# Moving the head norm's squared root to two idle buffers, and the last third of the rotation table into the value stage

## The chip, the core and the metric

The kernel runs on one core of one Trainium2 chip. The metric is the time of one execution on the device in microseconds (us); several runs are made and their median is given. Lower is better.

## What is computed

Four transformer layers in a row on 256 latent tokens and 256 context tokens of width 1024, all in 32-bit floats. The first layer, where most of the change acts, is cut here to what matters:

```python
def rms_norm(x, g):
    y = x * rsqrt(mean(x * x, axis=-1) + 1e-6)
    return y * g

# layer 0: neighbourhood attention; w = na_wqkv, 16 heads of 64
ql, kl, vl = split((u_lat @ w).reshape(B, L, 3, H, dh))
qc, kc, vc = split((u_ctx @ w).reshape(B, C, 3, H, dh))
ql, qc, kl, kc = (rms_norm(t, gain) for t in (ql, qc, kl, kc))   # per head of 64
# layer 1: sliding window attention, q and k normed per head in the same way, then rotated
# layer 2: s5_mixer, a diagonal complex state space model:
a_bar = exp(lam * dt)          # its powers, chunk by chunk, are the "rotations" below
```

The modulation vectors of layers 0 and 1 come from `silu(c) @ ada_w[i] + ada_b[i]`, a matrix-vector product with 96 slabs of 128 outputs each.

## The kernel before

Everything is written for the raw engines: each engine runs one list of instructions in order and waits on semaphores. The work is cut into **stages** (`make_plan`), each a matrix product whose output comes in tiles of 128 features. `qk0` makes the 16 query and key tiles of layer 0 over 512 tokens, `v0` its values in 8 weight units, then comes the attention of layer 0 (`ATT0`). `q1` (8 tiles of 256 tokens), `k1` (2 tiles of 512) and `v1` are the same for layer 1. A 32-bit product is three matmuls: operand and weight are each split into a high and a low part (L699 to L701; L764 to L766 in a value stage).

**A weight unit** (128x1024) is loaded by SyncE into one of four `raw` slots (L546). ScalarE copies it to `w_hi` (L1127, `split_unit`), VectorE makes `w_lo` (L1554, `lower`), three units ahead of TensorE.

**A query or key tile** of the stages `qk0`, `q1` and `k1` takes this path (`b2` is the tile's parity, for two sets of buffers):

1. ScalarE squares the bank of products into `sq[b2]` (L1145, "the Square").
2. TensorE sums the squares per head with a matmul against a constant (`sum_tile`, L777).
3. ScalarE: `tmp` from the sums (L1259), logarithm (L1131), exponential (L1132), which is the root `y` in `rs[b2]`, and the root squared (L1261), written to the same `sq[b2]` as the squares of step 1.
4. VectorE copies the products out (L1596) and applies one Newton step and the gain (`qk_scale`, L1748 to L1750). L1748 reads the squared root. Its end is semaphore `d2`.

Since the squared root of tile j lies in `sq[b2]` until L1748 has read it, the Square of tile j+2 waits for `d2` of tile j. ScalarE's order is: `w_hi` copy, Square of tile j, then the root (step 3) of tile j-1. The root of tile j waits for `d2` of tile j-2 as well, because of `tmp` and `rs`. TensorE's order in `qk0` and `q1` goes by groups of four tiles. Within a group the sum of a tile follows the products of the next one; at the group's end the sums of its last two tiles stand one behind the other, so the first product of the next group stands behind the last Square of this one.

**VectorE's list** in `qk0` has per tile: `lower`, a product of one `ada` slab for every second tile (`ada_unit`, L1566 and L1567), the copy and the Newton step, and one step of `rotations(u)`, u being the tile: the table `rot0` of powers for layer 2, doubled step by step (`rot_double`, L1978 to L1984). In `v0` it has `lower` and one or two `ada` slabs per unit. The `ada` slabs come through two buffers, each loaded again (L541) when its product is done. TensorE waits before the attention for the last `ada` product of `v0`, which writes to a bank that the attention uses.

**GpSimd** (POOL) only issues transfers here, in order: `pw` and `bbar` to DRAM, constants, `rot0` to DRAM (L2241, 1.5 MB), then 16 bias tiles for the attention (L2252): the first four when `qk0` is done, the others as the attention frees them. `rot0` lies where the attention puts its probabilities, so ScalarE waits for `pre_saved` (all three tables stored) before `v0`.

`rsn` and `ssum` are the buffers of the whole-row norm, which is not running while `qk0`, `q1` and `k1` do.

Of the kernel before, what the change touches and what calls it, by code (L numbers as in the profile page):

```python
# [154 lines left out]
def program(nc, weights, ada_w, ada_b, x_t, vecs, cons, bias_na, ssm_in, ssm_bc, scratch, out):  # L155
# [5 lines left out]
    with ctx:  # L161
# [39 lines left out]
        ssum = place("ssum", [P, TOK])  # L201
        tmp = place("tmp", [P, 2, TOK])
        half_eps = place("half_eps", [P, 1])
        whole_eps = place("whole_eps", [P, 1])
# [136 lines left out]
        ss0, x_in, pre_cout, pre_zero = sem("ss0"), sem("x_in"), sem("pre_ca_out"), sem("pre_zero")  # L341
        pre_saved, tab_loaded, bc_loaded, zero_set = sem("pre_saved"), sem("tab_loaded"), sem("bc_loaded"), sem("zero_set")
        gain_done = sem("gain_done")
# [767 lines left out]
        def _(act):  # L1111
# [4 lines left out]
            A = act.activation  # L1116
# [17 lines left out]
            def tile(s, i, jj, body, first=False):  # L1134
# [4 lines left out]
                if s.kind == "QK":  # L1139

                    act.wait_ge(S["unit"], n_done)
                    act.wait_ge(S["p2"], value("p2", s, j - 1))
                    if s.name not in LATE:
                        act.wait_ge(S["d2"], value("d2", s, j - 1))
                    A(sq[:, b2, 0:s.tok], bank[:, 0:s.tok], ACT.Square).then_inc(S["a1"], 1)  # L1145
# [106 lines left out]
            def qk_root(s, i, jj, body):  # L1252
                j = i * body + jj
                b2 = (s.tile0 + jj) % 2

                act.wait_ge(S["p2"], value("p2", s, j + 1))
                act.wait_ge(S["d2"], value("d2", s, j - 1))
                v, y = tmp[:, b2, 0:s.tok], rs[:, b2, 0:s.tok]
                chain.link(A(v, (SS, SS2)[b2][:, 0:s.tok], ACT.Identity, bias=half_eps[:, :], scale=-0.5 * INV_HD))  # L1259
                chain.link(root(y, v))  # L1260
                A(sq[:, b2, 0:s.tok], y, ACT.Square).then_inc(S["a2"], 1)  # L1261

# [184 lines left out]
            stage("qk0")  # L1447
            act.wait_ge(pre_saved, 48)
            stage("v0")
            attention(ATT0, 0)  # L1450
            stage("wo0"); norm(1, "mlp0")
# [88 lines left out]
        def _(dve):  # L1540
# [199 lines left out]
            def qk_scale(s, i, jj, body):  # L1740
# [5 lines left out]

                v, y, y2_ = tmp[:, b2, 0:s.tok], rs[:, b2, 0:s.tok], sq[:, b2, 0:s.tok]
                link(TT(v, v, y2_, ALU.mult))  # L1748
# [5 lines left out]
            def stage(name):  # L1754
# [10 lines left out]
                def one(i, first=False, last=False):  # L1765
                    for jj in range(body):
# [25 lines left out]
                        if s.name == "qk0":  # L1792
                            rotations(i * 4 + jj)
                    if s.kind == "QK" and s.name in LATE:
                        if i == 1:
                            late_mean(s, 7)
                            late_scale(s, 6)
                            late_scale(s, 7)
                    elif s.kind == "QK":
                        qk_scale(s, i, body - 1, body)  # L1800
# [185 lines left out]
            def rotations(u):  # L1986
# [13 lines left out]
                elif 4 <= u < 8:  # L2000
                    rot_double(2 ** (u - 4))
                elif u in (8, 9):
                    rot_double(16, re=(u == 8), im=(u == 9))
                elif u == 12:
                    link(dve.tensor_copy(rot0[:, 2, :, :], v(7).unsqueeze(2).to_broadcast([P, PAIRS, NCH])))
# [224 lines left out]
        def _(pool):  # L2230
# [8 lines left out]
            pool.dma_start(con[:, N_EARLY:], cons[:, N_EARLY:]).then_inc(late_in, 16)  # L2239
            pool.wait_ge(pre_v, 5)  # L2240
            pool.dma_start(rot_dram, rot0[:, :, :, :]).then_inc(pre_saved, 16)  # L2241
            chain = Chain(pool, pool_chain)
            link = chain.link

            for b in range(HEADS):
                if b == 0:

                    stage_end(pool, ST["qk0"], ("d2",))
                if b >= 4:
                    pool.wait_ge(att_m, 2 * (b - 4) + 2)  # L2250
# [8 lines left out]
            stage_end(pool, ST["up0b"], ("unit", "d1"))  # L2259
            pool.wait_ge(pre_saved, 48)  # L2260
            def table_inputs(H, js):
# [215 lines left out]
```

## Time and profile before

| | us |
|---|---|
| median of 3 runs | 1752.43 |
| lowest and highest run | 1748.91, 1753.97 |
| the profiled execution's own time | 1750.73 |
| its span (first to last instruction) | 1748.9 |
| mean granted TensorE clock, share of full speed | 0.968 |
| busy: TensorE matmul / VectorE / ScalarE | 1627.1 / 1312.5 / 870.6 |

The stages that the change touches lie in this stretch of the span: `qk0` from 44 to 162 us, `v0` from 162 to 208, the attention of layer 0 from 210; `q1` from 718 to 758, `k1` to 772, `v1` to 789, the attention of layer 1 from 792.

In the rows below PE is TensorE's matmul part, DVE is VectorE, ACT is ScalarE. A bracket at a row's end, `[1.99 <-DVE qk L1750]`, says how long the engine had been idle before the instruction and which instruction it had waited for. The idle time of an engine that nobody waits for costs nothing.

### The profile page before, as it was taken

Reading aid. Unit: us, or ns where it says so; the run is one execution under the profiler, and the core shown is the slowest. Engines: PE = TensorE matmul, PEld = TensorE weight load, DVE = VectorE, ACT = ScalarE, POOL = GpSimd, SP = SyncE. Lnnn points to the kernel's source line nnn. Section 1 sums busy time; section 2 is a strip of 40 time slices with the busy share of each in tenths; the row PEclk is TensorE's granted clock in tenths of the full one; section 3 lists DMA queues with packets and bytes.
Section 4 is the critical chain, followed back from the end, with each engine's and each line's share of the span. In section 5 each row is a group of like instructions: output and inputs, shape, how many; then the busy total and the mean of one; then the engine's idle time right before and its main releaser. Section 6 shows DMA issues by size and latency. Waiting matters only on the chain.

```text
span 1748.9 us, 32745 instructions
## 1 busy us (share of the span) xinstructions
PE 1627.1 (93%) x11892; PEld 1435.7 (82%) x11892; DVE 1312.5 (75%) x2239; ACT 870.6 (50%) x1497; POOL 96.5 (6%) x152
## 2 busy tenths in 40 slices
PE   5899999899999999698989999689999989799999
PEld 3677866688888888584789999689999988599999
DVE  4899797788767877678677786777887666468874
ACT  4555387343213433556555555155555576455552
POOL 0001030000000023100001212100000000000000
PEclk9899999999999999898999999799999999899999
DMA  9236651435657855320256768525555544045554
GB/s 359 87 108 228 217 140 43 145 119 187 200 192 239 264 177 167 106 94 13 66 183 203 220 200 304 234 97 174 186 180 192 183 143 145 1 156 180 182 192 142
DMA packets 79626, 290.74 MB, mean 166 GB/s; under 512 B 10000, under 2 KB 11792, under 8 KB 77600
## 3 DMA queue, kind: packets, MB, share of 16 engines
q1 hardware_dynamic: 69120, 249.03, 43.0%
q0 software_dynamic: 10400, 40.30, 7.0%
q8 instruction: 67, 1.10, 0.3%
q14 instruction: 39, 0.32, 0.1%
HBM read 270.61 MB, written 18.68 MB: 165 GB/s over the span
## 4 chain that ended last, share of the span: by engine, by line
PE 75%; DVE 14%; ACT 6%; issue 4%; DMA 2%; ACTq 0%; DVEq 0%; SPq 0%; POOLq 0%
PE bank L699 21%; PE bank L701 21%; PE bank L700 21%; DVE stat L2069 2%; PE bank L764 1%; PE bank L766 1%; PE bank L765 1%; ACT w_hi L1127 1%; DVE w_lo L1554 1%; DVE prob L2088 1%; DMA raw<-weights 1%; PE bank L909 1%; PE bank L920 1%; PE bank L777 1%; PE bank L933 1%
## 5 line engine op out<-in xcount | busy, mean ns | idle before, releaser
L699 PE MATMUL bank<-u_hi,w_hi 128*128 128x256 f32 (+1 forms) x1936 | 616.5, 318 | 36.3 <-DVE u_lo L1887 25.6
L700 PE MATMUL bank<-u_lo,w_hi 128*128 128x256 f32 (+1 forms) x1936 | 604.6, 312 | 0.0
L701 PE MATMUL bank<-u_hi,w_lo 128*128 128x256 f32 (+1 forms) x1936 | 604.3, 312 | 0.0
L1554 DVE TENSOR_TENSOR w_lo<-raw,w_hi 128x1024 fp32r<-128x1024 f32 x372 | 452.2, 1222 | 175.8 <-ACT w_hi L1127 163.3
L1127 ACT ACTIVATE w_hi<-raw 128x1024 fp32r<-128x1024 f32 x360 | 375.9, 1050 | 173.7 <-PE bank L701 144.6
L699 PEld LDWEIGHTS bank<-u_hi,w_hi 128*128 128x128 f32 x1936 | 376.6, 195 | 63.1 <-issue 39.2
L700 PEld LDWEIGHTS bank<-u_lo,w_hi 128*128 128x128 f32 x1936 | 376.6, 195 | 22.0 <-issue 3.0
L701 PEld LDWEIGHTS bank<-u_hi,w_lo 128*128 128x128 f32 x1936 | 376.1, 194 | 19.0
L699 PE MATMUL bank<-hid_hi,w_hi 128*128 128x512 f32 (+1 forms) x512 | 174.0, 340 | 0.0
L701 PE MATMUL bank<-hid_hi,w_lo 128*128 128x512 f32 (+1 forms) x512 | 172.1, 336 | 0.0
L700 PE MATMUL bank<-hid_lo,w_hi 128*128 128x512 f32 (+1 forms) x512 | 172.1, 336 | 0.0
L699 PEld LDWEIGHTS bank<-hid_hi,w_hi 128*128 128x128 f32 x512 | 97.2, 190 | 11.0 <-issue 1.5
L701 PEld LDWEIGHTS bank<-hid_hi,w_lo 128*128 128x128 f32 x512 | 97.1, 190 | 10.2
L700 PEld LDWEIGHTS bank<-hid_lo,w_hi 128*128 128x128 f32 x512 | 97.2, 190 | 9.7
L1567 DVE SCALAR_TENSOR_TENSOR ada_raw<-ada_raw,silu_row 128x1024 f32<-128x1024 f32 x80 | 97.6, 1222 | 8.5 <-DMA ada_raw<-ada_w 8.1
L699 PE MATMUL bank<-f_hi,w_hi 128*128 128x256 f32 x352 | 99.8, 283 | 0.0
L700 PE MATMUL bank<-f_lo,w_hi 128*128 128x256 f32 x352 | 99.6, 283 | 0.0
L701 PE MATMUL bank<-f_hi,w_lo 128*128 128x256 f32 x352 | 99.6, 283 | 0.0
L1180 ACT ACTIVATE rs<-bank 128x512 f32<-128x512 f32 (+1 forms) x64 | 31.4, 491 | 126.3 <-PE bank L701 119.8
L699 PEld LDWEIGHTS bank<-f_hi,w_hi 128*128 128x128 f32 x352 | 67.6, 192 | 0.2
L700 PEld LDWEIGHTS bank<-f_lo,w_hi 128*128 128x128 f32 x352 | 67.6, 192 | 0.0
L701 PEld LDWEIGHTS bank<-f_hi,w_lo 128*128 128x128 f32 x352 | 67.6, 192 | 0.0
(319 smaller groups left out, 2278.0 us busy)
## 6 DMA issues: line engine op xcount, KB each, us to landing
raw<-weights SPq DMA_DIRECT2D x372, 512.0 KB, 3.4
ada_raw<-ada_w SPq DMA_DIRECT2D x80, 512.0 KB, 4.2
ada_first<-ada_w SPq DMA_DIRECT2D x16, 512.0 KB, 15.5
bias_sb<-bias_na POOLq DMA_DIRECT2D x16, 256.0 KB, 3.3
toep_dram<-zeros POOLq DMA_DIRECT2D x8, 512.0 KB, 8.9
bat_dram<-bat POOLq DMA_DIRECT2D x16, 256.0 KB, 4.1
ca_dram<-ca POOLq DMA_DIRECT2D x16, 256.0 KB, 3.7
s_bat<-bat_dram POOLq DMA_DIRECT2D x4, 1024.0 KB, 7.5
```

The source lines that it names most:

```text
L699: pe.matmul(dst, wh, hi[:, kt, xs], start=first, stop=False)
L700: pe.matmul(dst, wh, lo[:, kt, xs], start=False, stop=False)
L701: return pe.matmul(dst, wl, hi[:, kt, xs], start=False, stop=final)
L764: pe.matmul(dst, hi[:, kt, xs], wh, start=first and tt % 2 == 0, stop=False, skip_group_check=True)
L765: pe.matmul(dst, lo[:, kt, xs], wh, start=False, stop=False, skip_group_check=True)
L766: mm = pe.matmul(dst, hi[:, kt, xs], wl, start=False, stop=final, skip_group_check=True)
L777: pe.matmul(SUM_BANKS[(s.tile0 + jj) % 2][:, 0:s.tok], C("block"), sq[:, (s.tile0 + jj) % 2, 0:s.tok], start=True, stop=True).then_inc(S[" ...
L1127: A(w_hi[:, slot, :], raw[:, slot, :], ACT.Copy).then_inc(S["hi"], 1)
L1180: chain.link(A(rs[:, b2, 0:s.tok], bank[:, 0:s.tok], ACT.Relu))
L1554: TT(w_lo[:, slot, :], raw[:, slot, :], w_hi[:, slot, :].bitcast(F32), ALU.subtract).then_inc(S["lo"], 1)
L1567: STT(raw_, raw_, 1.0, silu_row[:, 0, :], ALU.mult, ALU.mult, accum_out=ada_acc[:, b, a % 4, 0:1]).then_inc(S["ada_read"], 1)
L2069: red = dve.tensor_reduce(stat[:, 0, b, :], both[:, :, 0:keys], AX.X, ALU.max, negate=True)
```

## The change

1. The squared root (L1261) goes to `ROOT2[b2]`, that is `ssum` for even and `rsn` for odd tiles, and L1748 reads it there. With it the Square's wait for `d2` goes; its waits for TensorE's products and for the sum of tile j-2 stay.
2. `rotations` 8, 9 and 12 become 16, 17 and 18 and are called in the first three units of `v0`.
3. The store of `rot0` gets a semaphore of its own, `rot_saved`. GpSimd issues it behind the first four bias tiles; ScalarE waits for it behind `v0`, before the attention.

```diff
+        ROOT2 = (ssum, rsn)
...
                     act.wait_ge(S["p2"], value("p2", s, j - 1))
-                    if s.name not in LATE:
-                        act.wait_ge(S["d2"], value("d2", s, j - 1))
                     A(sq[:, b2, 0:s.tok], bank[:, 0:s.tok], ACT.Square).then_inc(S["a1"], 1)
...
-                A(sq[:, b2, 0:s.tok], y, ACT.Square).then_inc(S["a2"], 1)
+                A(ROOT2[b2][:, 0:s.tok], y, ACT.Square).then_inc(S["a2"], 1)
...
             stage("qk0")
-            act.wait_ge(pre_saved, 48)
+            act.wait_ge(pre_saved, 32)
             stage("v0")
+            act.wait_ge(rot_saved, 16)
             attention(ATT0, 0)
...
-                v, y, y2_ = tmp[:, b2, 0:s.tok], rs[:, b2, 0:s.tok], sq[:, b2, 0:s.tok]
+                v, y, y2_ = tmp[:, b2, 0:s.tok], rs[:, b2, 0:s.tok], ROOT2[b2][:, 0:s.tok]
...
                         if s.name == "qk0":
                             rotations(i * 4 + jj)
+                        if s.name == "v0":
+                            rotations(16 + i * 4 + jj)
...
-                elif u in (8, 9):
-                    rot_double(16, re=(u == 8), im=(u == 9))
-                elif u == 12:
+                elif u in (16, 17):
+                    rot_double(16, re=(u == 16), im=(u == 17))
+                elif u == 18:
...
             pool.dma_start(con[:, N_EARLY:], cons[:, N_EARLY:]).then_inc(late_in, 16)
-            pool.wait_ge(pre_v, 5)
-            pool.dma_start(rot_dram, rot0[:, :, :, :]).then_inc(pre_saved, 16)
...
+                if b == 4:
+                    pool.wait_ge(pre_v, 5)
+                    pool.dma_start(rot_dram, rot0[:, :, :, :]).then_inc(rot_saved, 16)
```

ScalarE, one tile inside `qk0`, before (`dve_second` is `d2`, `pe_heads` the sums, `act_chain` ScalarE's own order):

```order
L1127 ACTIVATE w_hi<-raw 128x1024 [waits unit_done,raw_in1]
L1141 REGISTER_ALU
L1145 ACTIVATE sq<-bank 128x512 [waits dve_second,pe_heads,unit_done]
L1259 ACTIVATE tmp<-bank,half_eps 128x512 [waits dve_second,pe_heads]
L390 REGISTER_ALU
L1131 ACTIVATE rs<-tmp 128x512 [waits act_chain]
L390 REGISTER_ALU
L1132 ACTIVATE rs<-rs 128x512 [waits act_chain]
L390 REGISTER_ALU
L1261 ACTIVATE sq<-rs 128x512 [waits act_chain]
```

and the same place now:

```order
L1128 ACTIVATE w_hi<-raw 128x1024 [waits unit_done,raw_in1]
L1142 REGISTER_ALU
L1144 ACTIVATE sq<-bank 128x512 [waits pe_heads,unit_done]
L1258 ACTIVATE tmp<-bank,half_eps 128x512 [waits dve_second,pe_heads]
L391 REGISTER_ALU
L1132 ACTIVATE rs<-tmp 128x512 [waits act_chain]
L391 REGISTER_ALU
L1133 ACTIVATE rs<-rs 128x512 [waits act_chain]
L391 REGISTER_ALU
L1260 ACTIVATE rsn<-rs 128x512 [waits act_chain]
```

No instruction moved; the Square lost one wait and the squared root has another target. The root's own wait for `dve_second` stays.

VectorE at the start of `v0`, before:

```order
L1554 TENSOR_TENSOR w_lo<-raw,w_hi 128x1024 [waits unit_hi]
L1566 SCALAR_TENSOR_TENSOR bank,ada_acc<-ada_raw,silu_row 128x1024 [waits ada_read,ada_in0]
L1567 SCALAR_TENSOR_TENSOR ada_raw,ada_acc<-ada_raw,silu_row 128x1024
L1554 TENSOR_TENSOR w_lo<-raw,w_hi 128x1024 [waits unit_hi]
L1566 SCALAR_TENSOR_TENSOR bank,ada_acc<-ada_raw,silu_row 128x1024 [waits ada_read,ada_in1]
```

and now:

```order
L1554 TENSOR_TENSOR w_lo<-raw,w_hi 128x1024 [waits unit_hi]
L1566 SCALAR_TENSOR_TENSOR bank,ada_acc<-ada_raw,silu_row 128x1024 [waits ada_read,ada_in0]
L1567 SCALAR_TENSOR_TENSOR ada_raw,ada_acc<-ada_raw,silu_row 128x1024
L1980 TENSOR_TENSOR rot_109<-rot_109 128x32x16
L1981 TENSOR_TENSOR rot_109<-rot_109 128x32x16 [waits dve_chain]
L1982 TENSOR_TENSOR rot_109<-rot_109 128x32x16 [waits dve_chain]
L1554 TENSOR_TENSOR w_lo<-raw,w_hi 128x1024 [waits unit_hi,dve_chain]
L1566 SCALAR_TENSOR_TENSOR bank,ada_acc<-ada_raw,silu_row 128x1024 [waits ada_read,ada_in1]
```

Three of the moved instructions stand behind the first `ada` product; three more follow behind the second, and a copy and a memset behind the third. They are gone from tiles 8, 9 and 12 of `qk0`.

GpSimd's list now, behind the constants:

```order
L2241 DMA con<-cons 128x1920 [waits unit_done]
L2255 DMA bias_sb<-bias_na 128x2x256 [waits dve_second]
L2255 DMA bias_sb<-bias_na 128x2x256 x3
L2251 DMA rot_dram<-rot_109 128x3072 [waits pre_small]
L2255 DMA bias_sb<-bias_na 128x2x256 [waits att_max] x12
```

The store of `rot0` stood ahead of the first bias tile and now stands behind the fourth.

## Rows read from the trace of the kernel before

**Rows 1.** The page's part 1: busy time and share of each engine.

```profile
PE 1627.1 (93%) x11892; PEld 1435.7 (82%) x11892; DVE 1312.5 (75%) x2239; ACT 870.6 (50%) x1497; POOL 96.5 (6%) x152
```

**Rows 2.** Windows: busy of PE, PEld, DVE, ACT, POOL, then clock, DMA share, GB/s.

```profile
62.00:169.00 107.00, 97.92 (x406) 73.91 (x405) 98.64 (x170) 65.69 (x97) 2.12 (x4) 0.94 0.43 147
134.00:138.00 4.00, 3.80 (x8) 2.40 (x9) 4.00 (x7) 3.84 (x8) 0.00 (x0) 0.58 0.44 141
```

**Rows 3.** Waits from 62 to 169 us: total, times, longest.

```profile
ACT sq L1145 <- DVE qk L1750: 11.6, 5, 5.6
```

**Rows 4.** Timeline (start, duration), ACT and PE at the first group's end.

```profile
71.33 0.60 ACT L1145 ACTIVATE sq<-bank 128x512 f32<-128x512 f32 x1 [1.99 <-DVE qk L1750]
...
76.84 0.60 ACT L1145 ACTIVATE sq<-bank 128x512 f32<-128x512 f32 x1 [1.41 <-DVE qk L1750]
...
77.49 2.07 PE L777 MATMUL bank<-sq,con 128*128 128x512 f32 x2 [3.89 <-ACT sq L1145]
78.58 1.42 PE L699 MATMUL bank<-u_hi,w_hi 128*128 128x512 f32 x1
...
82.75 0.40 PE L701 MATMUL bank<-u_hi,w_lo 128*128 128x512 f32 x1
```

**Rows 5.** Timeline, PE at the third group's end (tile 11), and beyond.

```profile
129.96 1.02 PE L777 MATMUL bank<-sq,con 128*128 128x512 f32 x2
134.20 2.07 PE L777 MATMUL bank<-sq,con 128*128 128x512 f32 x2 [3.21 <-ACT sq L1145]
135.28 1.42 PE L699 MATMUL bank<-u_hi,w_hi 128*128 128x512 f32 x1
...
137.34 0.39 PE L699 MATMUL bank<-u_hi,w_hi 128*128 128x512 f32 x1
```

**Rows 6.** Timeline, PE at the second group's end, where no wait is listed.

```profile
104.54 1.97 PE L777 MATMUL bank<-sq,con 128*128 128x512 f32 x4
106.09 0.66 PE L699 MATMUL bank<-u_hi,w_hi 128*128 128x512 f32 x1
...
107.05 0.40 PE L699 MATMUL bank<-u_hi,w_hi 128*128 128x512 f32 x1
107.28 0.39 PE L700 MATMUL bank<-u_lo,w_hi 128*128 128x512 f32 x1
```

**Rows 7.** Timeline, DVE, rotation step 8, what follows it, and step 12's copy.

```profile
119.00 0.68 DVE L1978 TENSOR_TENSOR rot<-rot 128x512 f32<-128x512 f32 x1
...
121.17 1.22 DVE L1554 TENSOR_TENSOR w_lo<-raw,w_hi 128x1024 fp32r<-128x1024 f32 x1
...
145.72 0.68 DVE L2005 COPY rot<-sv 128x1024 f32<-128x1024 f32 x1
```

**Rows 8.** Waits of DVE from 169 to 213 us.

```profile
DVE w_lo L1554 <- ACT w_hi L1127: 7.7, 6, 3.3
```

**Rows 9.** Timeline, the value stage: two DVE steps, and the attention's first matmul.

```profile
168.70 1.22 DVE L1554 TENSOR_TENSOR w_lo<-raw,w_hi 128x1024 fp32r<-128x1024 f32 x1
...
172.13 1.22 DVE L1554 TENSOR_TENSOR w_lo<-raw,w_hi 128x1024 fp32r<-128x1024 f32 x1
...
209.80 1.99 PE L909 MATMUL bank<-qk 64*128 64x512 f32 x8 [1.52 <-DVE ada_raw L1567]
```

**Rows 10.** The instructions on `ada_raw`, 44 to 215 us: landing of 18 loads.

```profile
DMA to landing us min/median/max: 3.2/3.3/8.3
```

**Rows 11.** DMA issues from 100 to 260 us: KB, us to landing.

```profile
rot_dram<-rot POOLq DMA_DIRECT2D x1, 1536.0 KB, 10.2
```

**Rows 12.** Timeline, stage q1: ACT at tiles 2 and 3, PE at both group ends.

```profile
736.74 0.38 ACT L1145 ACTIVATE sq<-bank 128x256 f32<-128x256 f32 x1 [0.83 <-DVE q L1750]
...
740.60 0.38 ACT L1145 ACTIVATE sq<-bank 128x256 f32<-128x256 f32 x1 [0.82 <-DVE q L1750]
...
741.03 1.22 PE L777 MATMUL bank<-sq,con 128*128 128x256 f32 x2 [3.16 <-ACT sq L1145]
...
757.55 0.70 PE L777 MATMUL bank<-sq,con 128*128 128x256 f32 x2 [1.30 <-ACT sq L1145]
```

More of the change, by code:

```diff
@@ L341, in program @@
         ss0, x_in, pre_cout, pre_zero = sem("ss0"), sem("x_in"), sem("pre_ca_out"), sem("pre_zero")
-        pre_saved, tab_loaded, bc_loaded, zero_set = sem("pre_saved"), sem("tab_loaded"), sem("bc_loaded"), sem("zero_set")
+        (pre_saved, rot_saved), tab_loaded, bc_loaded, zero_set = (sem("pre_saved"), sem("rot_saved")), sem("tab_loaded"), sem("bc_loaded"), sem("zero_set")
         gain_done = sem("gain_done")
@@ L2259, in _ @@
             stage_end(pool, ST["up0b"], ("unit", "d1"))
-            pool.wait_ge(pre_saved, 48)
+            pool.wait_ge(pre_saved, 32)
+            pool.wait_ge(rot_saved, 16)
             def table_inputs(H, js):
```

## The prediction

> **What bounds the kernel now.** The page's part 1 comes first [rows 1]: TensorE is busy for 93% of the span, VectorE for 75%, ScalarE for 50%. A change that removes no matmul can only win where TensorE stands idle or runs at half its clock. The window of the first stage shows where that is [rows 2]: from 62 to 169 us TensorE is busy 97.9 of 107.0 us at a granted clock of 0.94, and VectorE 98.6. Both are nearly full, so a wait between them is paid by both. The waits of that stretch name the one that the change removes [rows 3]: the Square of the products waited 5 times, 11.6 us in all, for VectorE's Newton step. The timeline then shows which of these five reach TensorE: those at the end of a group of four tiles, where TensorE has nothing but a sum to do. It stood idle 3.89 us before the sum of tile 3 [rows 4], 3.21 before the sum of tile 11 [rows 5], and in q1 3.16 and 1.30 [rows 12]. At the second group's end no wait is listed and the two sums and the next product follow at once [rows 6]. Waits of the Square inside a group are idle time of ScalarE that nobody waits for.
>
> **The change, part by part.**
>
> *The Square's wait, first group of qk0 (place A).* ScalarE's list between tile 1 and the sum of tile 3 is: copy, Square 2, root 1, copy, Square 3. Two waits for VectorE stand in it, 1.99 and 1.41 us [rows 4]. Both go, and nothing else in the list waits: tiles 2 and 3 are long done, and the root of tile 1 waits for no Newton step, there being no tile -1. So Square 3 ends 3.4 earlier, and with it the sum and the next product at 78.58. Gain 3.4. What is late next is Square 3 itself, behind a root and a weight copy. TensorE's idle of 3.89 before the last sum shrinks by less than 3.4, since the sum of tile 2 ends earlier too: laying the lists side by side leaves some 3 us of it.
>
> *The same, third group (place B).* TensorE ended tile 11's products and began sum 10 at 129.96; the first product of tile 12 came at 135.28, 5.32 later [rows 5]. At the second group's end the same distance is 106.09 - 104.54 = 1.55 [rows 6]. ScalarE loses two waits here too, enough to have Square 11 ready when tile 11 is. Gain 5.32 - 1.55 = 3.8.
>
> *The clock behind these gaps.* From 134 to 138 us the granted clock was 0.58 of full speed, that is mostly the 1.2 GHz level, behind an idle of 3.21 us [rows 2, 5]. Three products from 135.28 to 137.34 took 2.06 us; the same three behind the undisturbed end took 107.05 - 106.09 = 0.96 [rows 6]. So B gives back 1.1 more. Behind A eight products took 82.75 - 78.58 = 4.17 against 0.96 + 5 x 0.23 = 2.1 [rows 4, 6], a loss of 2.1. A keeps a gap of some 3 us, near B's, so I leave it B's loss of 1.1 and book 1.0. The bounds are 0 and 2.1. The Trainium skill (TensorE: Matmul & The Clock Gate, Part 1) says that the gate knows two levels only, and that how many matmuls run at the lower one differs from run to run of the same kernel. By that, this part of A may come out at either bound in any one execution: 1.0 less or 1.1 more than the sum below. No row here can decide it.
>
> *Stage q1 (places C and D).* The same list with tiles half as wide. Before the first group's last sum the Squares waited 0.83 and 0.82 us [rows 12]: gain 1.65. The second group's end had TensorE idle for 1.30 us, with the Squares ahead of it waiting in the same way: gain 1.3. The half clock behind C I leave unchanged, since some 2.5 us of the 3.16 remain. Sum 3.0. In k1 and v1 VectorE's rope steps follow the sums of k1 in one chain, so they start earlier by the same amount.
>
> *The squared root in rsn and ssum.* The same instructions with other addresses. I cost this at nothing; the buffers are idle here, and no instruction becomes longer.
>
> *The rotation steps.* A half of the doubling takes 121.17 - 119.00 = 2.17 us of VectorE [rows 7], two halves 4.3; the copy takes 0.68, and with memset and chain some 1.0. So 5.4 us leave qk0 and join v0. In qk0 they stand ahead of Newton steps for which the root, two tiles on, still waits. By laying the three lists side by side with these durations I find that without the move VectorE would just keep up; so the move is worth 0 beside the Square's edit, at most the 3.8 of place B if it alone had been made. What it buys is room: qk0 must now end 9.3 earlier, and VectorE has 8.4 idle [rows 2] and 5.4 of moved work, 13.8, to do so.
>
> *In v0.* VectorE runs from 168.70 to the last ada product, which released the attention's first matmul at 209.80 [rows 9]. In these 41 us it waited 7.7 for w_hi copies that hang on TensorE [rows 8]. Adding 5.4 leaves 2.3. So the cover holds, if narrowly; without it each microsecond delays the attention by one. Cost 0, at worst 5.4 if VectorE starts v0 with all its slack used.
>
> *GpSimd's order.* The four bias tiles now go ahead of the store of rot0. The store takes 10.2 us [rows 11]. Its data are ready behind the third step of v0, about 168.7 + 3 x 3.43 [rows 9] + 5.4 = 184 at the latest; it has landed by 195. The attention's first exponential cannot start before its scores, now at about 200. Cost of ScalarE's new wait: 0. The 12 later bias tiles wait for the attention anyway.
>
> **Sum:** 3.4 + 3.8 + 1.1 + 1.0 = 9.3 in qk0, 3.0 in q1, together 12.3. The profiled execution took 1750.73 us (its span is 1748.9), 1.7 below the median of the runs. On its footing the result is 1738.4, on the median's 1740.1. I give 1740. What changes the time by less than 0.3%, or 5.3 us, a measurement of this kernel can hardly tell from no change.
>
> **Rivals.**
>
> *1. VectorE paces qk0.* It is busy 98.6 of 107 us [rows 2]. The root of tile j still waits for the Newton step of tile j-2, the next Square stands behind the root, so the wait removed at the Square could come back there. Against it: it comes back two tiles later, and 13.8 us of room stand against 9.3. If VectorE gives back only half of its idle time and the 5.4 moved, the queue still shortens; if nothing but place B and its clock is won, with q1, the gain is 3.8 + 1.1 + 3.0 = 7.9: 1744.5. Chance 0.17.
>
> *2. The Square's wait was not the last.* Behind it stand the weight copy and the product's end. If TensorE's gaps stay as they are, only q1 gains: 1752.4 - 3.0 = 1749.4, no change that can be told. For it: the Square stands behind several things, and the profile names only the one that came last. Against it: rows 4 show the Square starting the moment that L1750 ended. Chance 0.08.
>
> *3. The ada loads become the bound of v0: slower.* The ada slabs have two buffers. A load starts when a product ends and is needed one step and a w_lo later, 3.43 + 1.2 = 4.6 us [rows 9]. The median landing is 3.3, the longest of 18 was 8.3 [rows 10]. Before, v0 shared the transfer engines with four bias tiles; now also with 1.5 MB of rot0, and VectorE has no slack to catch up. A pair of products costs 2 x 3.43 = 6.9 us while loads are early, and landing + 2.3 when they are late. With two pairs late at 8.3, 2 x 3.7 - 2.3 = 5.1 are given back: 1745.2; chance 0.08. All five pairs at the store's own 10.2 us would cost 5 x 5.6 - 2.3 = 25.7, a net loss of 13.4: 1765.8; chance 0.04. It ends slower than before by more than 0.3% once every load takes over 8.6 us, which none has. The Trainium skill (DMA: Bandwidth & Descriptors, Issuing engines are not separate DMA queues) speaks against the change here: transfers issued by SyncE and GpSimd run on the same 16 engines and interleave. By that rule the store lengthens the ada loads beside it, which is the 1745.2 of this rival if it holds for two pairs.
>
> **How the numbers follow.** Forecast 1740, chance 0.60, own range 1736 to 1744 (A's clock part at either bound, and 2 to 3 us between medians). Rival 1 has 0.17, rival 2 0.08, rival 3 0.08 and 0.04; 0.03 is for something unnamed. The range for 8 in 10 reaches from 1735.5, all half-clock time gone, to 1748.0, with rivals 1 and the milder 3 inside; rival 2 and the slower one, 0.12, lie outside, as do the tails. Faster by over 0.3% are the forecast, rival 1 and the milder rival 3, less their tails: 0.84. Within 0.3% is rival 2 and those tails: 0.11. Slower: 0.05.
>
> **What would show it.** After the change the Square waits for no L1750 at all. TensorE's idle before the sum of tile 3 falls from 3.89 to about 3, the shorter one before tile 2's sum goes, and so do the 3.21 before sum 11; in q1 the 1.30 goes and 3.16 becomes about 2.5. v0 starts some 9 us earlier, at about 152.5, the attention at about 200.5 instead of 209.8, still released by an ada product. VectorE's waits in v0 fall from 7.7 to about 3, and its six rotation instructions stand between 161 and 172. I am wrong if the root (L1258 in the new numbering) shows waits for VectorE of more than 2 us in sum, or if the attention of layer 0 starts after 203.

## The result and the profile after

| | before | after |
|---|---|---|
| median of the runs, us | 1751.66 (4 runs) | 1737.26 (4 runs) |
| lowest and highest run | 1748.91, 1753.97 | 1735.16, 1739.79 |
| profiled execution, its span | 1750.73, 1748.9 | 1737.44, 1735.7 |
| mean granted TensorE clock | 0.968 | 0.971 |

The ratio is 0.9924, with a 95% interval of 0.9912 to 0.9936: the changed kernel is faster by 14.4 us of median. A second round of five runs gave 0.993 (0.9916 to 0.9943). Forecast were 1740 us, in a range of 1735.5 to 1748.

The window of `qk0` in the changed kernel, beside [rows 2]; columns as there:

```profile
62.00:169.00 107.00, 104.13 (x466) 81.09 (x465) 99.24 (x170) 67.57 (x100) 4.46 (x7) 0.97 0.44 148
```

TensorE is busy for 104.1 of 107 us where it was busy for 97.9. VectorE is as full as before, 99.2 after 98.6, although its rotation steps are partly gone: the same list is pressed into less time, and the window now holds the first 13.5 us of `v0`, where it held 7.3 before. Keep that row in mind.

The waits of the same window (engine, tile and line; releaser; us in total, times, longest) say what became of [rows 3]:

```profile
ACT sq L1144 <- PE bank L702: 32.3, 13, 5.6
ACT tmp L1258 <- PE bank L778: 4.5, 10, 2.1
DVE tmp L1748 <- ACT rsn L1260: 2.5, 2, 2.1
```

The Square (now L1144) waits for TensorE alone, and no wait of the root (L1258) for VectorE is listed. The timeline of TensorE has places A, B and the end of `qk0` (start, duration, then as in [rows 4]):

```profile
75.71 2.07 PE L778 MATMUL bank<-sq,con 128*128 128x512 f32 x2 [2.87 <-ACT sq L1144]
76.79 1.41 PE L700 MATMUL bank<-u_hi,w_hi 128*128 128x512 f32 x1
78.00 0.63 PE L701 MATMUL bank<-u_lo,w_hi 128*128 128x512 f32 x1
...
81.84 0.43 PE L701 MATMUL bank<-u_lo,w_hi 128*128 128x512 f32 x1
...
128.68 1.97 PE L778 MATMUL bank<-sq,con 128*128 128x512 f32 x4
130.20 0.68 PE L700 MATMUL bank<-u_hi,w_hi 128*128 128x512 f32 x1
...
154.11 1.97 PE L778 MATMUL bank<-sq,con 128*128 128x512 f32 x4
```

Place B's gap [rows 5] is gone altogether: the two sums and the next product follow at once, 1.52 us in all. At place A an idle of 2.87 us is left of 3.89, and behind it products of 0.63 us, which is the 1.2 GHz level, run until 81.84. ScalarE's own timeline shows why 2.87 is left:

```profile
71.08 0.58 ACT L1144 ACTIVATE sq<-bank 128x512 f32<-128x512 f32 x1
...
74.13 1.04 ACT L1128 ACTIVATE w_hi<-raw 128x1024 fp32r<-128x1024 f32 x1
75.08 0.58 ACT L1144 ACTIVATE sq<-bank 128x512 f32<-128x512 f32 x1
```

Square 2 and Square 3 wait for nobody now; between them stand the root of tile 1 and a weight copy. The engine that was waiting before is now simply late. In `q1`, beside [rows 12]:

```profile
730.19 0.70 PE L778 MATMUL bank<-sq,con 128*128 128x256 f32 x2 [0.92 <-ACT sq L1144]
733.11 0.70 PE L778 MATMUL bank<-sq,con 128*128 128x256 f32 x2 [2.23 <-ACT sq L1144]
747.49 1.34 PE L778 MATMUL bank<-sq,con 128*128 128x256 f32 x4
```

The 3.16 became 2.23, the 1.30 of the second group is gone. In `v0`, VectorE's rotation steps, its longest wait for an `ada` load, and TensorE's first matmul of the attention, which stand against [rows 8, 9]:

```profile
166.00 0.68 DVE L1980 TENSOR_TENSOR rot<-rot 128x512 f32<-128x512 f32 x1
...
173.05 0.69 DVE L1986 TENSOR_TENSOR rot<-rot 128x512 f32<-128x512 f32 x1
...
188.33 1.23 DVE L1566 SCALAR_TENSOR_TENSOR bank<-ada_raw,silu_row 128x1024 f32<-128x1024 f32 x1 [2.95 <-DMA ada_raw<-ada_w]
...
203.88 1.99 PE L910 MATMUL bank<-qk 64*128 64x512 f32 x8 [1.72 <-DVE ada_raw L1567]
```

VectorE's 7.7 us of waits for `w_hi` in `v0` are gone. In their place stand the moved steps and a wait of 2.95 us for a load, which was not there before. The moved steps are not the only thing that took the 7.7 away: in e1 and e9 below, where nothing is moved into `v0`, 0.7 and 3.2 us of them are left. There VectorE's list was the same as before and only `qk0` had become shorter.

### The profile page after: what moved, and what is told of

It is laid out like the page before. It is cut to its first block, busy times and chain, and to the rows that moved or that the text cites. A ratio compares the mean times of both kernels' runs of the same rounds, so it can differ in the third digit from the quotient of the medians.

```text
span 1735.7 us, 32739 instructions
## 1 busy us (share of the span) xinstructions
PE 1622.9 (94%) x11892; PEld 1432.8 (83%) x11892; DVE 1310.7 (76%) x2239; ACT 870.9 (50%) x1497; POOL 96.5 (6%) x152
## 4 chain that ended last, share of the span: by engine, by line
PE 74%; DVE 13%; ACT 5%; issue 4%; DMA 3%; SPq 1%; ACTq 0%; DVEq 0%
PE bank L700 22%; PE bank L701 22%; PE bank L702 22%; DVE stat L2071 2%; ACT w_hi L1128 1%; DVE prob L2090 1%; DVE w_lo L1554 1%; DMA raw<-weights 1%; PE bank L778 1%; PE bank L910 1%; DMA ada_first<-ada_w 1%; SPq L535 1%; PE bank L921 1%; PE bank L934 1%; DMA ada_raw<-ada_w 1%
```

## Where the time went, stage by stage

Distances between marks in TensorE's timeline, in us. The second execution of the changed kernel is that of experiment e5, below.

| from - to | before | after | after, 2nd | gain, forecast |
|---|---|---|---|---|
| first product of `qk0` - first behind A | 34.56 | 31.55 | 30.59 | 3.0, 4.0 / 3.4 |
| - sums at the second group's end | 25.96 | 26.45 | 24.01 | -0.5, 2.0 / 1.0 |
| - first product behind B | 30.74 | 26.96 | 26.93 | 3.8, 3.8 / 3.8 |
| - sums at the end of `qk0` | 24.96 | 23.91 | 23.87 | 1.1, 1.1 / 1.1 |
| - first matmul of the attention (`v0`) | 49.56 | 49.77 | 50.67 | -0.2, -1.1 / 0 |
| `q1`, first product behind sum 0 - attention of layer 1 | 58.9 | 55.4 | 56.4 | 3.4, 2.4 / 3.0 |

So `qk0` with `v0` gained 7.1 and 9.7 us (9.3 forecast), `q1` 3.4 and 2.4. Of the first execution's 13.2 us of span, 10.6 lie there, and 1.2 were lost ahead of `qk0`, whose first product came at 45.24 and not at 44.02 (44.08 in the second). The rest lies where nothing was changed. From the first matmul of layer 1's attention to the end of the span took 957.3 us before, 953.6 after and 956.2 in the second execution; over all the kernels below it is 953.6 to 958.4. One profile thus can't book a gain of 2 or 3 us there to anything. For the same reason the 14.4 us of the median can't be laid to the touched stages in full: the two profiles find 10.6 and 12.1 of it there.

## The experiments

**The Square's edit alone (e1, and again as e9).** The kernel before, with `ROOT2` and without the wait; rotations and store stay in `qk0`.

```diff
-                    if s.name not in LATE:
-                        act.wait_ge(S["d2"], value("d2", s, j - 1))
...
-                A(sq[:, b2, 0:s.tok], y, ACT.Square).then_inc(S["a2"], 1)
+                A(ROOT2[b2][:, 0:s.tok], y, ACT.Square).then_inc(S["a2"], 1)
```

> The kernel before with the Square's edit alone: the squared root in rsn and ssum, no wait of the Square for d2; the rotation steps and the store of rot0 stay in qk0. My theory: the wait at the Square held TensorE, and VectorE just keeps up without the move, so places A, B, C and D all go as in the changed kernel: 1738 to 1740 us, within 2 us of it, no idle of TensorE over 1 us at tile 11, attention of layer 0 starting at about 204 us. Rival: VectorE paces qk0 and only the moved steps make room, so place B's 3.8 and its 1.1 of half clock stay: 1742 to 1743 us, and the wait turns up at the root (L1258) or as TensorE idle before sum 11.

> The Square's edit alone once more, beside the two below. It ran at 1735.7 us where the whole change ran at 1737.3 and 1738.1, and the pair with the reordered list differed by 3.0 in the same direction. If moving the last third of the rotation table costs 1.5 to 3 us, this is again 1735 to 1736.5 us; if the difference was chance, 1737 to 1738.5.

Measured: 1735.66 us (ratio 0.991, 0.9896 to 0.9925), and again 1734.17 (0.99, 0.9885 to 0.9915). The timeline of TensorE in the first of them:

```profile
73.77 1.12 PE L778 MATMUL bank<-sq,con 128*128 128x512 f32 x2 [2.87 <-ACT sq L1144]
...
123.75 1.97 PE L778 MATMUL bank<-sq,con 128*128 128x512 f32 x4
125.28 0.68 PE L700 MATMUL bank<-u_hi,w_hi 128*128 128x512 f32 x1
...
198.76 1.99 PE L910 MATMUL bank<-qk 64*128 64x512 f32 x8 [1.57 <-DVE ada_raw L1566]
```

B's gap is gone without the move. One edit makes the whole gain, and more: eight runs of it average 1735.1 us, nine runs of the whole change 1737.8, with a standard error of 0.6 each. They come from several chips, on which the kernel before had medians of 1750.8 to 1751.7. So the move of the rotation steps and the store buys no time and by these averages costs 2.7 us.

It does what it was meant to do all the same. The root's wait for VectorE from 62 to 169 us in e1:

```profile
ACT tmp L1258 <- DVE qk L1749: 8.0, 6, 3.3
```

The wait taken from the Square came back at the root, as the rival had it, 8.0 us of it (1.4 in e9); in the changed kernel it is 0, and 0.4 in its second execution. But TensorE stood idle no longer for it in e1: it fell into time in which ScalarE had waited for TensorE anyway (the Square's waits for products are 23.8 us there and 32.3 in the changed kernel).

**The wait put back (e2).** The changed kernel, with the Square's wait (the two removed lines of the diff above) restored.

> The changed kernel with one line put back: the Square waits for d2 again, though the squared root stays in rsn and ssum and the rotations stay in v0. My theory: the wait is what cost the time, the buffers by themselves nothing, and the move alone is worth at most place B's 3.8 and 1.1 of clock: 1746.8 to 1751.7 us, TensorE idle about 3.9 before the sum of tile 3 and 3.16 and 1.30 in q1, as before. Rival: the moved rotation steps (5.4 us of VectorE) made the gain, the wait was incidental: 1738 to 1742 us.

Measured: 1748.24 us (0.998, 0.9972 to 0.9989), 2.6 us below the kernel before. TensorE's timeline, and the Square's wait from 62 to 169 us:

```profile
77.92 2.08 PE L778 MATMUL bank<-sq,con 128*128 128x512 f32 x2 [4.02 <-ACT sq L1146]
```

```profile
ACT sq L1146 <- DVE qk L1752: 8.9, 5, 3.4
```

The buffers alone are worth nothing: A's gap is 4.02 again. The move alone shortens VectorE's queue, so that B's gap falls from 3.21 to 0.52 and `qk0` ends 4.1 us earlier, but `v0` then takes 1.4 us longer, and the median keeps 2.6. The median lies in my theory's range and far from the rival's: the wait was the cause.

**The edit in `qk0` only (e3).** The wait stands again for `q1` and `k1`.

```diff
+                    if s.name in ("q1", "k1"):
+                        act.wait_ge(S["d2"], value("d2", s, j - 1))
```

> The changed kernel with the Square's wait put back in q1 and k1 alone. My theory: q1 gives back the 3.5 us that its stretch gained in the profile after (from its first product to the attention of layer 1: 73.2 before, 69.7 after): 1740 to 1741.5 us, idle of 3.16 and 1.30 back. Rival: the profile's 3.5 was a matter of the clock of one execution and q1 gives only its listed waits or less: under 1739 us.

Measured: 1740.84 us (0.9945, 0.9932 to 0.9958), 3.2 above the mean of the changed kernel's medians (1737.26 and 1738.07): `q1`'s part of the gain, as my theory had it. From its first product to the attention of layer 1 `q1` took 73.0 us, against 69.7 in the changed kernel and 73.2 before. The idle of `q1` is back as it was:

```profile
730.88 1.22 PE L778 MATMUL bank<-sq,con 128*128 128x256 f32 x2 [3.16 <-ACT sq L1146]
```

**More VectorE work in `v0` (e4).** The two halves of the last doubling are done twice, 4.3 us.

```diff
                             rotations(16 + i * 4 + jj)
+                            if i == 0 and jj < 2:
+                                rotations(16 + jj)
```

> The changed kernel with the two moved halves of the last doubling done twice in v0: six more VectorE instructions, 4.3 us. It measures the cover in v0. My theory: VectorE's remaining waits in v0, 1.0 for w_hi and 3.1 for ada loads, cover most of it: attention 0.2 to 1.5 us later than in the changed kernel, 1737.5 to 1739 us. Rival: v0 has no cover left, its waits for loads are there whatever VectorE does, and the attention starts 3.3 to 4.3 us later: 1740.5 to 1741.5 us.

Measured: 1744.54 us (0.9957, 0.9945 to 0.9969), 6.9 above the changed kernel. My theory missed, and the rival with it, by 3 us the other way. VectorE's wait and TensorE's first matmul of the attention:

```profile
192.56 1.23 DVE L1566 SCALAR_TENSOR_TENSOR bank<-ada_raw,silu_row 128x1024 f32<-128x1024 f32 x1 [2.98 <-DMA ada_raw<-ada_w]
```

```profile
208.06 3.62 PE L910 MATMUL bank<-qk 64*128 64x512 f32 x8 [6.06 <-DVE ada_raw L1567]
```

TensorE waits 6.06 us for the last `ada` product in place of 1.72: all 4.3 came through. The wait of 2.95 us that I had counted as cover did not shrink, it moved along (188.33 to 192.56). It hangs on the store, which GpSimd issues when the steps are done, so more steps push store, load and wait back together: the store was issued at 178.44 us in the changed kernel and at 182.64 here, and with the store out of `v0` (e12, below) the wait is gone. The other 2.6 us of the median lie outside the stage. The profile has 0.9 of them between the attention's first matmul and `q1` (behind the long idle the first eight matmuls took 3.62 us and not 1.99) and 1.1 in `q1`, as much as lies between the two executions of the changed kernel; the rest stays unexplained.

**The store alone moved (e10).** The Square's edit, the steps in `qk0`, and only the store behind the first four bias tiles.

```diff
-            pool.wait_ge(pre_v, 5)
-            pool.dma_start(rot_dram, rot0[:, :, :, :]).then_inc(pre_saved, 16)
...
+                if b == 4:
+                    pool.wait_ge(pre_v, 5)
+                    pool.dma_start(rot_dram, rot0[:, :, :, :]).then_inc(rot_saved, 16)
```

> The Square's edit, the rotation steps left in qk0, and only the store of rot0 moved behind the first four bias tiles with its own semaphore. It tells which half of the move costs. If the store, by landing among the ada loads of v0 (waits of VectorE for ada loads of 3 us or more in place of 1.7, attention later by 1 to 2 us): 1737 to 1739 us. If the steps in v0, by standing ahead of its ada products: within 1 us of the Square's edit alone, 1735 to 1736.5 us. I hold the store for the likelier, since the one long wait for an ada load (2.8 to 3.3 us in every profile with the move) falls within the store's 10 us.

Measured: 1741.31 us (0.9954, 0.994 to 0.9967), 7.1 above e9 from the same chip and above both of my ranges. VectorE's wait, TensorE's first matmul of the attention, the store's landing from 155 to 200 us, and the landings of the `ada` loads from 155 to 210 us:

```profile
176.96 1.23 DVE L1566 SCALAR_TENSOR_TENSOR bank<-ada_raw,silu_row 128x1024 f32<-128x1024 f32 x1 [5.26 <-DMA ada_raw<-ada_w]
```

```profile
203.40 3.78 PE L910 MATMUL bank<-qk 64*128 64x512 f32 x8 [5.96 <-DVE ada_raw L1567]
```

```profile
rot_dram<-rot POOLq DMA_DIRECT2D x1, 1536.0 KB, 9.9
```

```profile
DMA to landing us min/median/max: 3.6/4.3/9.9
```

Two `ada` loads beside the store took 9.8 and 9.9 us to land, where the longest of `v0` was 5.4 in e1 and 6.5 in the changed kernel. `v0` took 54.0 us instead of 49.6. So a store in `v0` can hold its loads up, but this is not the price that it has in the changed kernel, since it doesn't lie at the same place. Here the table is long done, so the store follows the four bias tiles at once; there it waits for the steps and is issued 12.6 us later. GpSimd's timeline in e10, then in the changed kernel:

```profile
166.89 0.56 POOL L2249 DMA_DIRECT2D rot_dram<-rot  x1
```

```profile
178.44 0.56 POOL L2251 DMA_DIRECT2D rot_dram<-rot  x1 [12.62 <-DVEq L2009]
```

The two slow loads were issued at 167.2 and 170.6 us, beside the store and right behind the bias tiles, which GpSimd issued from 164.0 on. How much of the 4.4 us is the store's, and how much that of the two together, no run tells.

**The steps alone in `v0` (e12).** The changed kernel with the store back in `qk0`, zeros in the half of the table that isn't made yet, and the store behind the bias tiles taken out. VectorE's steps and the attention wait for the store and the table by a line each; neither wait shows in the trace.

```diff
+            link(pool.memset(rot0[:, :, :, 16:NCH], 0.0))
+            pool.dma_start(rot_dram, rot0[:, :, :, :]).then_inc(rot_saved, 16)
```

> The changed kernel with its rotation steps in v0 as they are, but with the store of rot0 back in qk0, ahead of the bias tiles. The stored table then lacks its last half (it holds zeros there, set by GpSimd), so this kernel leaves out that part of the layer 2 computation; the steps, the loads and the sizes are all the same. It takes the store out of v0 and leaves the steps. If the store beside the ada loads is what makes the whole change 2 to 3 us slower than the Square's edit alone: no ada wait of 2.8 us in v0, 1733.5 to 1736 us. If the steps in v0 are: 1737 to 1738.5 us, with the store's absence changing nothing.

Measured: 1738.38 us (0.9934, 0.992 to 0.9948). In the profile VectorE waits for no `ada` load from 147 to 209 us and `v0` takes 49.56 us, as before. The time says the second case, the trace of `v0` the first. So the 2.7 us between the whole change and its one half don't lie in `v0`, or only in part. One more place shows a difference: from the first matmul of layer 0's attention to the first product of `q1` the four profiles with the Square's edit and without the move (e1, e9, and e8 and e11 below) took 507.0 to 507.9 us, those of the changed kernel 508.5 and 508.7, e12 508.6. But the kernel before, which has no move either, took 508.6 too, so the move isn't shown to be the cause. Where the 2.7 us come from stays open.

**The changed kernel again (e5).**

> The changed kernel again, unaltered, as the measure for the three below. Expected 1737.3 us, between 1735 and 1740. What its profile is to tell: whether the half clock behind place A (the first product after the sum of tile 3 to the first sum of tile 7 took 26.5 us in the profile after, 24.0 in the two executions that stood at full clock there) belongs to this kernel or to the execution. If to the kernel, 26.5 again; if to the execution, it may be either.

Measured: 1738.07 us (0.993, 0.9916 to 0.9943). Place A and the attention:

```profile
74.10 1.13 PE L778 MATMUL bank<-sq,con 128*128 128x512 f32 x2 [2.87 <-ACT sq L1144]
74.67 0.79 PE L700 MATMUL bank<-u_hi,w_hi 128*128 128x512 f32 x1
...
200.15 1.99 PE L910 MATMUL bank<-qk 64*128 64x512 f32 x8 [2.62 <-DVE ada_raw L1567]
```

The same idle of 2.87, and no half clock behind it: the first product takes 0.79 and not 1.41. It belongs to the execution.

**ScalarE's order in the first group (e6).** What kept Square 3 late at A is the order of ScalarE's list. Here the first group of `qk0` and `q1` is written out by itself:

```diff
+                split_unit(s, 0, 0, body * s.units); square(0)
+                split_unit(s, 0, 1, body * s.units); square(1)
+                split_unit(s, 0, 2, body * s.units); square(2)
+                qk_root(s, 0, 0, body)
+                qk_root(s, 0, 1, body, between=lambda: square(3))
+                split_unit(s, 0, 3, body * s.units)
+                qk_root(s, 0, 2, body)
+                qk_root(s, 0, 3, body)
```

`between` stands behind the root's first instruction, which frees the bank of the sums.

> The changed kernel with ScalarE's list in the first group of qk0 and q1 in another order: Square 2 ahead of root 0, Square 3 behind the first instruction of root 1 (the one that frees the sums' bank, which the sum of tile 3 now waits for by a semaphore of its own). The idle of 2.87 us before the sum of tile 3, and 0.92 and 2.23 in q1, should fall below 0.7 each. My theory: at the attention of layer 0 TensorE waits for VectorE's last ada product, so VectorE's work up to there is the bound and what qk0 gains is lost at the attention, TensorE's wait for ada growing from 1.7 to about 4; only q1's 2.2 to 4 (with its half clock) stay: 1733.0 to 1735.5 us. Rival: TensorE is still the bound, qk0's gap is won too: 1728.5 to 1732 us.

Measured: 1733.67 us (0.9906, 0.9891 to 0.9921), within what the theory gave. TensorE's timeline:

```profile
69.95 1.97 PE L781 MATMUL bank<-sq,con 128*128 128x512 f32 x4
71.36 0.80 PE L700 MATMUL bank<-u_hi,w_hi 128*128 128x512 f32 x1
...
116.96 0.50 PE L700 MATMUL bank<-u_hi,w_hi 128*128 128x512 f32 x1 [1.53 <-DVE w_lo L1581]
...
199.56 3.78 PE L913 MATMUL bank<-qk 64*128 64x512 f32 x8 [3.57 <-DVE ada_raw L1594]
```

A's gap is gone and the next product comes 3.3 us earlier than in e5. Of these, 1.5 are given back where TensorE now waits for VectorE's `w_lo`, and the attention starts only 0.6 earlier, with TensorE idle for 3.57. VectorE is the bound there. What `q1` gained, where VectorE has room, stays: its stretch up to the attention of layer 1 took 66.0 us against 70.7 in e5 and 69.7 in the first profile.

**Room for VectorE (e7, e8, e11).** In e7 the rotation steps 0 to 2 stand ahead of tile 0's copy, where VectorE had been idle for 5.0 us. In e8 the rest of the steps and the store are back in `qk0` as well. In e11 the last `ada` product of `v0` moves to `wo0`.

```diff
+                        if s.name == "qk0" and i * 4 + jj == 0:
+                            for u in range(3):
+                                rotations(u)
...
-        Stage("v0", "V", 8, tok=TOK, ada=(1, 1, 1, 2) * 2),
-        Stage("wo0", "RES", 8, tok=TOK, ada=(1,) * 6 + (0, 0), norm=True, gate=(0, 2)),
+        Stage("v0", "V", 8, tok=TOK, ada=(1, 1, 1, 2, 1, 1, 1, 1)),
+        Stage("wo0", "RES", 8, tok=TOK, ada=(2,) + (1,) * 5 + (0, 0), norm=True, gate=(0, 2)),
```

> The same, and VectorE's rotation steps 0, 1 and 2 (4.8 us) moved ahead of the copy of tile 0, where VectorE stood idle for 5.0 us. My theory: this gives VectorE the room that the reordered list needs, so the attention of layer 0 starts 2.5 to 5 us earlier than in the kernel with the new order alone: 1728 to 1731.5 us. Rival (TensorE the bound, VectorE's room worth nothing): within 1 us of the kernel with the new order alone.

> The same as the last, but with the last doubling, its copy and the store of rot0 in qk0 as in the kernel before, so that neither the rotation steps nor the 1.5 MB store fall into v0. My theory: the sum of VectorE's work ahead of the attention is the same, and the loads of ada in v0 land sooner without the store beside them (one waited 2.95 us in the profile after), so it is 0 to 2.5 us faster than the last: 1726.5 to 1731 us. Rival: with 5.4 us more of VectorE in qk0 the roots wait for Newton steps and a gap opens at a group's end: 1 to 4 us slower than the last.

> The fastest so far (reordered first group, rotation steps 0 to 2 early, the rest and the store in qk0) with the last ada product of v0 moved to the first unit of wo0. VectorE's last two products before the attention of layer 0 shrink by 2.4 us and a load wait of 0.4. Theory that VectorE's list is the bound there: TensorE's idle of 1.84 before the attention goes and the attention starts 1.5 to 2.8 us earlier, 1725.5 to 1727.5 us. Rival: something else is the last there (the eviction of the values), or wo0 pays: 1728 to 1729.5 us.

Measured: e7 1731.4 us (0.9894, 0.9879 to 0.9909), e8 1728.38 (0.9878, 0.9863 to 0.9893), e11 1726.9 (0.9868, 0.9852 to 0.9883). The first matmul of the attention in the three:

```profile
196.69 1.99 PE L913 MATMUL bank<-qk 64*128 64x512 f32 x8 [2.83 <-DVE ada_raw L1594]
```

```profile
196.39 1.99 PE L913 MATMUL bank<-qk 64*128 64x512 f32 x8 [1.84 <-DVE ada_raw L1593]
```

```profile
196.21 1.99 PE L913 MATMUL bank<-qk 64*128 64x512 f32 x8 [1.27 <-ACT val L1166]
```

Counted from the first product of `qk0`, e7's attention starts 2.6 us earlier than e6's by nothing but VectorE's list, as the theory had it. In e11 the releaser is for the first time not VectorE but ScalarE's copy of the values, so VectorE has stopped being the bound. Its attention starts 0.6 us earlier than e8's, counted in the same way, where I had expected 1.5 to 2.8: the next wait stood close behind. The intervals of e8 and e11 overlap, so their difference of 1.5 us isn't established. That e7 to e8 is 3.0 us again says that the last third of the table is better left in `qk0`. e11 keeps the computation whole and is the fastest: 24.4 us less than the kernel before on the same chip, 10.0 more than the 14.4 of the change.

## Why the prediction was right, and where it was not

*What bounds the kernel, and the Square's wait.* Right. e1, e2 and e3 show the wait as the cause in both stages, and the buffers as free (e2: idle 4.02 at A).

*Place A, 3.4.* The wait itself gave 3.6: from the sum of tile 0 to that of tile 3 it took 12.85 us before and 9.22 in both executions after. The table's 3.0 and 4.0 hold other things besides: 0.6 us lost ahead of tile 0's sum in the first execution, 0.5 us of full clock behind the sum of tile 3 in the second. Some 3 us of idle were to be left; it was 2.87 in each profile with this order of ScalarE's list and without the wait.

*Place B, 3.8, and its clock, 1.1.* 3.8 and 1.1, in both executions. Taking the undisturbed second group as the measure was right to a tenth of a microsecond.

*The clock behind A, 1.0 with bounds of 0 and 2.1.* In the first profile it was -0.5, below my lower bound, in the second 2.0, at the upper one. The mistake was the lower bound: I had taken the half clock behind before's gap as the worst case, and a shorter gap can be followed by a longer stretch. The Trainium skill (TensorE: Matmul & The Clock Gate, Part 1) says of the start of a kernel that the number of matmuls at the lower level differs from run to run of one kernel; in the two executions the same holds for a gap in its middle.

*`q1`, 3.0.* 3.4 and 2.4. The 2.5 that were to be left at C were 2.23, the 1.30 went. The half clock behind C, which I left unchanged, was there in both executions; in the second it began earlier, with the sum of tile 3 itself (1.22 us for 0.70), and the 1.0 us between them lies there: from this sum to that of tile 4 it took 7.8 and 8.8 us.

*The rotation steps: no gain beside the Square's edit.* Right in that (e1). At most 3.8 if alone: `qk0` gained 4.1 in e2. "What it buys is room" came true and was wrong as an argument for it. The room is there (the root's 8.0 us of waits in e1 are 0 and 0.4 with the move), but TensorE wasn't waiting for it. And moved work is still ahead of the attention, and the attention waits for the end of VectorE's list. I had counted VectorE's room in `qk0` by itself, when the list up to the last `ada` product is one.

*`v0`, cost 0, and GpSimd's order, cost 0.* These are the two steps that failed, with 0.2 and 1.1 us in the trace. I subtracted 5.4 from 7.7 and took the 2.3 left for cover. e4 shows that none was left: 4.3 more of work delayed the attention by 4.3. Part of the 7.7 had gone to the shorter `qk0` already, as e1 shows (0.7 left without any moved step). For the store I asked only whether ScalarE would have to wait for it, and it didn't; its price is that it lies beside the `ada` loads. e10 shows how high it can get when the store meets the bias tiles too, 4.4 us in `v0`. The trace of before already had a sign of it. I had read 8.3 us as the longest of 18 landings; it is the one load that was issued at 150.29 us, while the store of `rot0` (issued at 146.94, 10.2 us to landing) was on its way in `qk0`, where nobody waited for it. The load among the issues from 150 to 153 us:

```profile
ada_raw<-ada_w SPq DMA_DIRECT2D x1, 512.0 KB, 8.3
```

This was rival 3. I gave its mild form 0.08, at a net cost of 5.1 us; its mechanism is in both profiles of the changed kernel as one wait of 2.95 or 2.80 us, nearly all of it absorbed by what the `w_hi` waits had been. The Trainium skill (DMA: Bandwidth & Descriptors, Issuing engines are not separate DMA queues) says that transfers issued by SyncE and by GpSimd run on the same engines; these landings, 8.3 and 9.9 us against a median of 3.3 before and 4.3 in e10, agree with it.

*Rival 1, VectorE paces `qk0`.* It didn't in the changed kernel, as the waits of the root show. Without the move the wait did come back at the root (e1), and TensorE didn't feel it. VectorE is the bound that comes next: 3.3 us more taken out of `qk0` (e6) brought the attention 0.6 forward. *Rival 2* fell with e2.

*What would show it.* The Square's waits, the idles at A, B, C and D, the steps' place (166.0 to 173.7 us) and the releaser of the attention came as written. `v0` began at 155.5 and 150.9 us where I had said 152.5, and the 3 us of VectorE's waits that were to remain in `v0` were 3.1 and 3.5, but for loads and not for `w_hi`. I had said that I would be wrong if the attention started after 203: it started at 203.88, and at 200.15 in the second execution. The absolute mark held 1.2 us of the lead-in and 2.5 of clock that are not the change's; a distance from the first product of `qk0` would have been the better mark.

*The sum, 12.3.* The touched stages gained 10.6 and 12.1. That the second comes so near is in part luck: the 1.1 of `v0` and the 0.6 missing in `q1` are made up by 1.0 more of clock and 0.6 more at A. The 14.4 of the median holds some 2 us more, which no stage shows.

## What to carry to other kernels

A wait that an engine has for a buffer is worth what the bound engine stands idle behind it. The nearest undisturbed place in the same trace is a good measure of that; here it was right to a tenth of a microsecond. The longest landing of a load is worth a look at what was on its way beside it. Waits of an engine are no cover until it is known what they hang on: one that hangs on a load that hangs on a store that hangs on the work just moved will move with the work. And before work is shifted from one stage to the next, look for the point behind both where its engine is waited for; only moving it past that point, or into idle time ahead of the first wait, makes room. Room is worth nothing, though, where the bound engine doesn't wait for it.

## What the runs showed of the hardware

The same idle of 2.87 us before the same sum was followed by half clock in four profiles and by full clock in four. It went with the lead-in: where the first product of `qk0` came at 44.8 to 45.4 us (after, e4, e9, e12) half clock followed, where it came at 43.9 to 44.1 (e1, e3, e5, e10) full clock. The windows around A in the profile after and in e5:

```profile
75.00:83.00 8.00, 7.29 (x17) 5.09 (x18) 7.72 (x17) 6.65 (x11) 0.00 (x0) 0.57 0.34 115
```

```profile
73.00:81.00 8.00, 6.90 (x28) 5.37 (x29) 7.72 (x15) 7.23 (x12) 0.00 (x0) 1.00 0.33 96
```

The two ways of running differ by 1.2 us ahead of `qk0` and by some 2.5 behind A. Why an execution takes one or the other no run here tells. With the Square's wait in place, and so a longer idle at A (3.89 us before, 4.02 in e2), half clock followed although the first product came at 44.0 and 44.4 us. The list without the gap (e6, e7, e8, e11) ran at full clock there every time, but three of these four profiles had the early lead-in (43.9 to 44.1), with which the clock stayed full behind the gap as well, and e11 lies between (44.5). So they don't show what the gap costs in clock.

The first eight matmuls of layer 0's attention took 1.99 us in the eleven profiles in which TensorE had been idle for 1.27 to 2.93 us before them. In the other three, with 3.57 (e6), 5.96 (e10) and 6.06 us (e4), they took 3.6 to 3.8 us, at a granted clock of 0.50 to 0.58 over four microseconds. A wait there cost up to 1.8 us more than its own length.
